# Stick-breaking attention: queries on partitions and a scan on VectorE, in place of keys on partitions and matmuls with triangles

## The reference

```
z        = q k^T / sqrt(128)
log_keep = log_sigmoid(-z)              where j < i, else 0
suffix   = sum of log_keep over the keys behind j (j+1 ... i-1)
a        = exp(log_sigmoid(z) + suffix) where j < i, else 0
out      = a v
```

## Time and profile before

| what | value |
|---|---|
| median of 3 runs | 2907.09 us (2906.19 to 2908.72) |
| the profiled execution, its own time | 2909.09 us |
| its span, first to last instruction | 2907.3 us |
| TensorE matmul busy | 2857.2 us, 98% |
| VectorE busy | 1243.0 us, 43% |
| ScalarE busy | 976.7 us, 34% |
| GpSimd busy | 1164.9 us, 40% |
| granted TensorE clock, mean | 0.994 |

### The profile page before, as it was taken

How to read it: one execution, slowest core, us unless ns; L and a number is a source line. 1 busy time by engine, 2 the same in 40 slices (tenths; PEclk the granted TensorE clock), 3 DMA queues, 4 the chain that set the end, 5 groups by cost and what they waited for, 6 DMA issues and landing times.

```text
span 2907.3 us, 41207 instructions
## 1 busy us (share of the span) xinstructions
PE 2857.2 (98%) x16960; PEld 2454.5 (84%) x16960; DVE 1243.0 (43%) x2194; ACT 976.7 (34%) x1433; POOL 1164.9 (40%) x888
## 2 busy tenths in 40 slices
PE   8999999999999999999999999999999999999997
PEld 8999999999999999777878778778878787788775
DVE  6333333333333358344434353532423244355546
ACT  4323222222223235344242344432332322234442
POOL 4343334333342434343434337434444343344342
PEclk9999999999999999999999999999999999999998
DMA  4222222222222212222222224222222221222221
GB/s 179 71 87 73 88 73 73 87 74 78 82 73 73 88 66 88 87 73 73 87 73 87 75 107 160 87 73 87 86 74 87 73 92 69 87 87 77 87 87 73
DMA packets 36942, 247.42 MB, mean 85 GB/s; under 512 B 3970, under 2 KB 4115, under 8 KB 8212
## 3 DMA queue, kind: packets, MB, share of 16 engines
q1 hardware_dynamic: 35728, 241.36, 23.6%
q10 hardware_dynamic: 1028, 3.44, 0.3%
HBM read 240.59 MB, written 4.19 MB: 84 GB/s over the span
## 4 chain that ended last, share of the span: by engine, by line
PE 87%; DVE 6%; ACT 2%; DVEq 2%; DMA 1%; POOL 1%; issue 1%; ACTq 0%; SPq 0%
PE pj L301 20%; PE pj L307 19%; PE pj L305 19%; PE pj L362 3%; PE pj L366 3%; PE pj L364 3%; PE pj L1136 2%; PE pj L1138 2%; PE pj L1137 2%; PE pa L543 1%; PE pa L505 1%; POOL wl L2259 1%; PE pa L1067 1%; ACT wh L273 1%; DVE arena L445 1%
## 5 line engine op out<-in xcount | busy, mean ns | idle before, releaser
L2259 POOL TENSOR_TENSOR wl<-raw,wh 128x512 fp32r<-128x512 f32 x884 | 1164.7, 1349 | 1707.2 <-ACT wh L273 1707.0
L301 PE MATMUL pj<-xh,wh 128*128 128x264 f32 (+2 forms) x3728 | 1082.9, 336 | 2.7 <-POOL wl L2259 1.5
L307 PE MATMUL pj<-xh,wl 128*128 128x264 f32 (+2 forms) x3728 | 1048.7, 327 | 0.0
L305 PE MATMUL pj<-xl,wh 128*128 128x264 f32 (+2 forms) x3728 | 1047.1, 327 | 0.0
L273 ACT ACTIVATE wh<-raw 128x2048 fp32r<-128x2048 f32 x221 | 423.1, 1914 | 990.8 <-PE pj L307 637.0
L301 PEld LDWEIGHTS pj<-xh,wh 128*128 128x128 f32 x3728 | 633.3, 189 | 80.1 <-issue 21.3
L305 PEld LDWEIGHTS pj<-xl,wh 128*128 128x128 f32 x3728 | 632.0, 188 | 60.6 <-issue 5.6
L307 PEld LDWEIGHTS pj<-xh,wl 128*128 128x128 f32 x3728 | 632.4, 189 | 60.1
L388 DVE TENSOR_TENSOR acc<-pj,acc 128x528 f32<-128x528 f32 (+1 forms) x192 | 134.2, 700 | 127.3 <-PE pj L366 126.3
L362 PE MATMUL pj<-oh,wh 128*128 128x264 f32 (+1 forms) x640 | 180.0, 330 | 2.7 <-DVE acc L388 1.1
L366 PE MATMUL pj<-oh,wl 128*128 128x264 f32 (+1 forms) x640 | 177.6, 326 | 0.0
(11 more groups left out here) (317 smaller groups left out, 2752.3 us busy)
## 6 DMA issues: line engine op xcount, KB each, us to landing
raw<-in_stream SPq DMA_DIRECT2D x221, 1024.0 KB, 4.8
acc<-in_x SPq DMA_DIRECT2D x8, 528.0 KB, 10.3
out_y<-acc SPq DMA_DIRECT2D x8, 512.0 KB, 2.9
arena<-in_mem ACTq DMA_DIRECT2D x2, 1024.0 KB, 6.2
cst<-in_cst SPq DMA_DIRECT2D x1, 448.0 KB, 13.7
cos<-in_cos_a SPq DMA_DIRECT2D x1, 264.0 KB, 13.8
sin<-in_sin_a SPq DMA_DIRECT2D x1, 264.0 KB, 14.1
cos<-in_cos_b ACTq DMA_DIRECT2D x1, 264.0 KB, 2.8
```

The costliest lines, as they stand in the source:

```text
L301: pe.matmul(pj[:, pu, b, 0:m], whk, xh[:, k, a:a + m], start=(k == 0), stop=False)
L305: pe.matmul(pj[:, pu, b, 0:m], whk, xl[:, k, a:a + m], start=False, stop=False)
L307: ins = pe.matmul(pj[:, pu, b, 0:m], wlk, xh[:, k, a:a + m], start=False, stop=(k == KD - 1))
L2259: pool.tensor_tensor(wl[:, j, at], raw[:, j, at], wh[:, j, at].bitcast(F32), ALU.subtract).then_inc(s_part if c < LO_PARTS - 1 else s_lo, 1)
```

## The change

Scores are made with queries on partitions: for each block of 128 queries one matmul over all keys up to its own block (again 1280 columns). VectorE now adds a mask of -1e30 to the four diagonal blocks in PSUM (`mask`), ahead of ScalarE's Abs, Exp, Ln. The value projection is taken out next. `weights` then makes softplus in `S_sp`, runs one `tensor_tensor_scan` per block of queries over 128, 256, 384 and 512 keys from the last key to the first, in place (state = max(state + x, x)), and writes z minus that sum to `S_e`. ScalarE takes Exp. `sb_c` and the block sums are gone; in their place `sb_tr` makes ten 128 x 128 transposes on TensorE at tile 2, k = 14 (tile 5 for the second head), into `pa`, and ScalarE waits for them and copies 1280 columns into `S_eT` (the memory of `S_sp`), from which `sb_pv` reads. The triangles after the Exp and three squares of `cst` are gone.

```diff
--- before.py
+++ after.py
@@ -112,9 +112,9 @@
         o_parts = (ohb[:, 0:2, :], olb[:, 0:2, :])
         o_last = (ohb[:, 2:4, :], olb[:, 2:4, :])
         o_in_x = (xsh[:, KD - 2:KD, :], xsl[:, KD - 2:KD, :])
-        cst = sb("cst", 7 * P)
-
-        ident, ones, tri, strict, neg_low, neg_ones, tri64 = (cst[:, i * P:(i + 1) * P] for i in range(7))
+        cst = sb("cst", 4 * P)
+
+        ident, ones, tri, tri64 = (cst[:, i * P:(i + 1) * P] for i in range(4))
         par = sb("par", NPAR)
         cos = sb("cos", T)
         sin = sb("sin", T)
@@ -207,8 +207,8 @@
         s_qk = sem("s_qk")
         s_z = sem("s_z")
         s_l = sem("s_l")
-        s_sp = sem("s_sp")
-        s_c = sem("s_c")
+        s_zm = sem("s_zm")
+        s_tr = sem("s_tr")
         s_am = sem("s_am")
         s_ae = sem("s_ae")
         s_a = sem("s_a")
@@ -1454,16 +1454,17 @@
         S_on = sb("S_on", 2)
         S_off = [0, SEQ, SEQ + 384 + P, SEQ + 384]
 
-        S_behind = [S_q[:, 0:3 * P], S_k[:, 0:2 * P], S_sp[:, S_off[3]:S_off[3] + P]]
+        S_zoff = [SEQ + 384, SEQ + 384 + P, SEQ, 0]
+        S_eT = S_sp
         S_scale = float(P) ** -0.5
 
         def sb_z(n):
             def f(pe):
                 pe.wait_ge(s_qk, 3 * n + 2)
-                for i in (0, 1, 3, 2):
-                    w = SEQ - P * i
-                    ins = pe.matmul(pa[:, S_off[i]:S_off[i] + w], S_k[:, P * i:P * (i + 1)], S_q[:, P * i:SEQ],
-                                    start=(i != 3), stop=False, skip_group_check=True)
+                for i in range(NQ):
+                    w = P * (i + 1)
+                    ins = pe.matmul(pa[:, S_zoff[i]:S_zoff[i] + w], S_q[:, P * i:P * (i + 1)], S_k[:, 0:w],
+                                    start=True, stop=True, skip_group_check=True)
                 ins.then_inc(s_z, 1)
             return f
 
@@ -1475,18 +1476,14 @@
                 ins.then_inc(s_vt, 1)
             return f
 
-        def sb_c(n):
+        def sb_tr(n):
             def f(pe):
-                pe.wait_ge(s_sp, n + 1)
+                pe.wait_ge(s_ae, n + 1)
                 for i in range(NQ):
-                    w = SEQ - P * i
-                    ins = pe.matmul(pa[:, S_off[i]:S_off[i] + w], neg_low, S_sp[:, S_off[i]:S_off[i] + w],
-                                    start=False, stop=(i == NQ - 1), skip_group_check=True)
-                    if i < NQ - 1:
-
-                        ins = pe.matmul(pa[:, S_off[i] + P:S_off[i] + w], neg_ones, S_behind[i], start=False,
-                                        stop=True, skip_group_check=True)
-                ins.then_inc(s_c, 1)
+                    for kb in range(i + 1):
+                        at = S_off[kb] + P * (i - kb)
+                        ins = pe.transpose(pa[:, at:at + P], S_e[:, S_zoff[i] + P * kb:S_zoff[i] + P * (kb + 1)], ident)
+                ins.then_inc(s_tr, 1)
             return f
 
         def sb_pv(n, H):
@@ -1495,15 +1492,15 @@
                 pe.wait_ge(s_vn, n + 1)
                 pe.wait_ge(s_oe, H + 1)
                 for i in range(NQ):
-                    ins = pe.matmul(bank[3][:, P * i:SEQ], S_vn[:, i, :], S_e[:, S_off[i]:S_off[i] + SEQ - P * i],
+                    ins = pe.matmul(bank[3][:, P * i:SEQ], S_vn[:, i, :], S_eT[:, S_off[i]:S_off[i] + SEQ - P * i],
                                     start=(i == 0), stop=(i == NQ - 1))
                 ins.then_inc(s_pv, 1)
             return f
 
         def sb_pe(pe, p):
             t, u, n = T_SB + 1 + SB_TILES * p, U_SB + 1 + SB_OUTS * p, 2 * p
-            hooks = {1: {8: [sb_z(n)]}, 2: {6: [sb_vt(n)], 12: [sb_c(n)]}, 3: {10: [sb_pv(n, n)]},
-                     4: {2: [head_ss_pe(n, S_sq)], 8: [sb_z(n + 1)]}, 5: {6: [sb_vt(n + 1)], 12: [sb_c(n + 1)]},
+            hooks = {1: {8: [sb_z(n)]}, 2: {6: [sb_vt(n)], 14: [sb_tr(n)]}, 3: {10: [sb_pv(n, n)]},
+                     4: {2: [head_ss_pe(n, S_sq)], 8: [sb_z(n + 1)]}, 5: {6: [sb_vt(n + 1)], 14: [sb_tr(n + 1)]},
                      6: {5: [sb_pv(n + 1, n + 1)], 10: [head_ss_pe(n + 1, S_sq)]}}
 
             for j in range(8):
@@ -1518,7 +1515,7 @@
                 if j in (1, 4):
                     if j == 4:
                         head_rs_act(act, n, S_rs)
-                    act.wait_ge(s_z, n + a + 1)
+                    act.wait_ge(s_zm, n + a + 1)
                     act.activation(S_e, pa[:, 0:S_ZW], ACT.Abs)
                     act.drain()
                     act.activation(S_e, S_e, ACT.Exp, scale=-1.0)
@@ -1529,6 +1526,8 @@
                     act.activation(S_vn, as3(bank1, NQ), ACT.Copy).then_inc(s_vn, 1)
                     act.wait_ge(s_am, n + a + 1)
                     act.activation(S_e, S_e, ACT.Exp).then_inc(s_ae, 1)
+                    act.wait_ge(s_tr, n + a + 1)
+                    act.activation(S_eT, pa[:, 0:S_ZW], ACT.Copy).then_inc(s_a, 1)
                 if j == 3:
                     head_sq_act(act, n, S_o[:, 0, :], S_sq)
                 if j == 5:
@@ -1544,31 +1543,23 @@
             u, n = U_SB + 1 + SB_OUTS * p, 2 * p
             dve.tensor_copy(S_on[:, :], par[:, PCOL["out_norm"]:PCOL["out_norm"] + SB_HEADS][:, bass.ds(n, 2)])
 
-            def softplus(n):
+            def mask(n):
+                dve.wait_ge(s_z, n + 1)
+                for i in range(NQ):
+                    d = pa[:, S_zoff[i] + P * i:S_zoff[i] + P * (i + 1)]
+                    dve.scalar_tensor_tensor(d, tri, NEG, d, ALU.mult, ALU.add)
+                dve.drain()
+                dve.sem_inc(s_zm, 1)
+
+            def weights(n):
                 dve.wait_ge(s_l, n + 1)
                 dve.scalar_tensor_tensor(S_sp, pa[:, 0:S_ZW], 0.0, S_e, ALU.max, ALU.add)
                 dve.drain()
                 for i in range(NQ):
-                    d = S_sp[:, S_off[i]:S_off[i] + P]
-                    dve.tensor_tensor(d, d, strict, ALU.mult)
+                    x = S_sp[:, S_zoff[i]:S_zoff[i] + P * (i + 1)][:, ::-1]
+                    dve.tensor_tensor_scan(x, x, x, 0.0, ALU.add, ALU.max)
                 dve.drain()
-
-                for i in (1, 0):
-                    own = S_sp[:, S_off[i + 1]:S_off[i + 1] + SEQ - P * (i + 1)]
-                    dve.tensor_copy(S_behind[i][:, 0:P], own[:, 0:P])
-                    dve.tensor_tensor(S_behind[i][:, P:], own[:, P:], S_behind[i + 1], ALU.add)
-                    dve.drain()
-                dve.sem_inc(s_sp, 1)
-
-            def weights(n):
-                dve.wait_ge(s_c, n + 1)
-                dve.tensor_scalar(S_e, pa[:, 0:S_ZW], 0.0, None, ALU.min).then_inc(s_am, 1)
-                dve.wait_ge(s_ae, n + 1)
-                for i in range(NQ):
-                    d = S_e[:, S_off[i]:S_off[i] + P]
-                    dve.tensor_tensor(d, d, strict, ALU.mult)
-                dve.drain()
-                dve.sem_inc(s_a, 1)
+                dve.scalar_tensor_tensor(S_e, S_sp, -1.0, pa[:, 0:S_ZW], ALU.mult, ALU.add).then_inc(s_am, 1)
 
             def read_out(n, o):
                 dve.wait_ge(s_pv, n + 1)
@@ -1585,7 +1576,7 @@
                 dve.sem_inc(s_qk, 2)
                 if a == 1:
                     head_norm_dve(dve, n, S_o[:, 0, :], S_on[:, 0:1], S_rs)
-                softplus(n + a)
+                mask(n + a)
                 evac_scaled(dve, S_v, u + 3 * a + 1, (3 * a + 2) % 2, SEQ).then_inc(s_evac, 1)
                 dve.drain()
                 dve.sem_inc(s_qk, 1)
@@ -2464,12 +2455,11 @@
     ca, sa = rope_tables(P // 4, [0])
     cb, sb_ = rope_tables(16, [0, 64])
     r = np.arange(P)
-    cst = np.concatenate([np.eye(P), np.ones((P, P)), (r[:, None] <= r[None, :]), (r[:, None] < r[None, :]),
-                          -1.0 * (r[:, None] >= r[None, :]), -np.ones((P, P)),
+    cst = np.concatenate([np.eye(P), np.ones((P, P)), (r[:, None] <= r[None, :]),
                           (r[:, None] <= r[None, :]) & (r[:, None] // 64 == r[None, :] // 64)], 1).astype(f)
     x0 = np.concatenate([i["x"][0], i["meta_tokens"]], 0).T
     return {"cst": cst, "par": par, "cos_a": ca, "sin_a": sa, "cos_b": cb, "sin_b": sb_,
-            "tri4": np.concatenate([cst[:, 6 * P:]] * 4 + [cst[:, 2 * P:3 * P]] * 4, 1),
+            "tri4": np.concatenate([cst[:, 3 * P:]] * 4 + [cst[:, 2 * P:3 * P]] * 4, 1),
             "mem": np.ascontiguousarray(feat(i["mem_2"][0].T)),
             "w_up": np.concatenate([i["w_gla_gate_up_2"][0], i["b_gla_gate_2"]], 0),
             "w_sgu": np.ascontiguousarray(i["w_sgu_2"][0].transpose(2, 0, 1)),
```

## The result

The changed kernel takes 2912.53 us (median of 16 runs, 2909.16 to 2915.73) against 2908.53 us of the kernel before in runs beside it: ratio 1.0016, 95% interval 1.0009 to 1.0022, that is 2.6 to 6.4 us slower. (One of the 16 runs of the kernel before took 15833.93 us; the other 15 lie between 2904.03 and 2911.08, and the median does not depend on it.) The forecast was 2923. The measured time lies inside the stated range, but the move, 4.0 us, is a quarter of the one forecast (15.9) and within what I had called no change. The profiled execution took 2912.06 us, 3.0 more than the one before.

What follows compares the result with a forecast made beforehand. TensorE was taken to bound the eight-head stage; per head -3.46 + 1.11 + 2.7 (wait) + 1.7 (clock) = +2.05 us, +16.4 in eight, against 2907.09: 2923 us. Range for 8 in 10: 2887 to 2928.

Steps and rivals of the forecast that it cites:

- What bounds the stage, and TensorE's work: Eight-head stage: TensorE's instructions set the time; sums removed -3.46 us, ten transposes +1.11, net -2.35 us per head without waits.
- The mask is covered: Four mask instructions ahead of ScalarE's Abs, 1.1 us, cost nothing: the wait for tile 1 covers them, 0.5 us over.
- The scans alone: Four scans without GpSimd: 1.33 us of columns at one step each, or 2.67 at two; the upper was taken.
- The rival with one step per column: Scans take one step per column, chain 1.33 us shorter, wait 1.4 us: -0.95 us per head, 2899.5; chance 0.1.
- The turns with GpSimd: Scans alternate with GpSimd's four weight instructions, ending at 1886.75, so TensorE waits 2.7 us per head ahead of the transposes.
- the rival without turns: Scans don't take turns with GpSimd, so the chain ends before the transposes: full 2.35 us gained per head, 2888; chance 0.2.
- What follows the transposes: Behind the transposes, ScalarE's copy of 1.24 us and the next `hi_part`, then `sb_pv`: nothing delayed, no cost.
- What the wait does to the clock: Behind each 2.7 us TensorE wait the clock falls to 0.50 for 3.4 us, losing 1.7 us per head.
- TensorE waits, but its clock stays up: Rival: TensorE waits ahead of the transposes without a low clock following: +0.35 us per head, 2910; chance 0.15.

Runs made afterwards that it cites:

- k = 12: The changed kernel with the transposes two blocks earlier in TensorE's list, gaps of 3.63 us ahead of them: 2930.02 us, ratio 1.0077.

## Why the prediction was wrong

By its own steps:

- *What bounds the stage, and TensorE's work:* right. -3.46 us is borne out by the run without the sums (27.7 us in eight heads), +1.11 by the run with z in PSUM (1.11). Score matmuls, value transposes and weighted sums cost the same in both kernels (2.16, 0.44 and 2.16 us in each head, by the distance between starts).
- *The mask is covered:* right. 0.89 us for the four; ScalarE's Ln ends at 1877.2 and `hi_part` starts at 1877.88, as soon as tile 1 is through, with 0.66 us over (0.5 forecast).
- *The scans alone:* right at the upper of its two bounds, 2.08 ns per column. The Trainium skill's half throughput ("DVE: opcode table, instruction layouts, handler registers and perf-mode slots", section 6) agrees. The rival with one step per column is out.
- *The turns with GpSimd:* right. The chain from GpSimd's start to the last scan's end was 7.24 us where I had 7.63, since a turn of GpSimd is nearer 1.1 than 1.19 us; so the wait was 2.49 us and not 2.7. That both inputs are the same memory, which spoke for the rival without turns, changes nothing. The rival without turns is out for this form, and what it would have given, 2888, is what the form with one input in PSUM does give (2886.8). The Trainium skill ("SBUF — State Buffer", Who interferes with whom) says that a VectorE instruction with two inputs in SBUF contends with a GpSimd instruction that reads SBUF, and that one with at most one SBUF input, outside the 2-port modes, doesn't. Both halves are seen here: 6.90 us with two inputs in SBUF, 2.96 with one.
- *What follows the transposes:* right; no new gap stands behind them, in the changed kernel or in the one with the transposes still later.
- *What the wait does to the clock:* this is the step that failed. I wrote 1.7 us "in each head in which it happens" and summed it over all eight, 13.6 us, from two gaps of 1.93 and 2.35 us that were followed by a low clock and one of 1.37 that was not. It took two cases for a rule. Three heads of eight fell, and they cost 4.9 us, 0.6 per head and not 1.7; with it the stage lost 6.0 us where I had 16.4. The other gaps of the nine traces say the same: behind the unchanged gap of 1.93 us the clock fell in 3 of 9 traces, and behind the three unchanged gaps of 2.33 to 2.39 us (lines 1412 and 1687 of the kernel before) in 13 of 27. The rival "TensorE waits, but its clock stays up", 2910 with a chance of 0.15, came closest in time, but that is luck in part: the clock did fall in three heads, and what they cost was given back elsewhere. The lower end of my own range named the case, "the clock falls in about half of the heads", and put it at 2916.
- *A step that was missing:* I compared the change with a kernel that I took to lose nothing to the clock elsewhere. Its profile had six low stretches, five in TensorE's work and one at its end; the changed kernel's had six too, three of them new in the stage, and the three that the kernel before had behind the stage were not there. Between two profiles only the difference is paid. No run shows the change as the reason why those three were missing: outside the stage and the end, the nine traces have between one and five, with no order by kernel. The 3.0 us between the profiles are 1.1 of work and wait, 0.8 from ahead of the stage, 0.1 between the three low stretches paid and the three given back, and 1.0 from line 470 at the lower clock. Over 16 runs the difference is 4.0 us (2.6 to 6.4), 1.1 of it work and wait. The rest fits the clock: its mean is 0.9936 over these 16 runs and 0.9950 over the 22 runs of the kernel before beside the experiments, which on 2910 us is an estimated 4 us of full-speed time, the end included. How this divides between the stage and the rest of the kernel is not shown.

What stays open: why, of equal gaps in one trace, some are followed by a low clock and some are not. At k = 12, with gaps alike to 0.04 us, the clock fell 2.0 to 4.1 us after TensorE had stopped, so the length is not all that decides. Where in time the gap lies is an obvious candidate; moving the transposes changes that place along with the length, and shifting gaps of one length in time was not tried by itself.

## What to carry to other kernels

When VectorE has to work beside GpSimd's SBUF instructions, count its inputs in SBUF: with two, each instruction also waits for one of GpSimd's (0.8 to 1.05 us here). If one input can be taken from PSUM, or replaced by something already there, the price goes (6.90 to 2.96 us for these four scans). A change that takes work from the bounding engine and lengthens a chain to it is worth what its slot in that engine's list allows: the same kernel is 0.5% slower or 0.7% faster than before with the transposes one block earlier or four blocks later. A gap on TensorE of 2 to 3 us should be priced with a share of a low clock stretch (here 3 of 8 at 2.28 us and 6 of 8 at 2.96), not with none and not with a whole one, and against the low stretches that the kernel has already.

## What the runs showed of the hardware that was not expected

- The share of gaps that are followed by 3.4 us at a granted clock of 0.50 grows with their length: 0 of 8 at 1.6 us, 3 of 8 at 2.28 (twice), 6 of 8 at 2.96, 8 of 8 at 3.63. Gaps elsewhere in the nine traces: 3 of 9 at 1.93, 13 of 27 at 2.33 to 2.39. (The gap of 2.45 to 2.55 us ahead of line 470 is left out: only two matmuls follow it, and the clock is low at the end of all nine traces.) Behind one gap of 3.65 us the low stretch lasted 6.8 us.
- A low clock can come without any gap: in the kernel before it was 0.50 from 2700.3 to 2703.7 us behind 3.2 us of short fp32 matmuls (128 columns, half of them from a single partition) in which TensorE never stood idle. Such a run of matmuls stands in four places of the kernel; in the nine traces 9 of the 36 were followed by a low stretch.
- A scan reads and writes backwards in place at the pace of a forward one, 1.22 us for 512 columns.
